# Reordering four short schedules around retention and the first merge tiles of a hybrid decoder step

## The chip, the core and the metric

The program runs on one core of a Trainium2 chip, in float32. The core has a matrix engine (TensorE, PE in the profile), a vector engine (VectorE, DVE), an activation engine (ScalarE, ACT), a general engine (GpSimd, POOL) and a queue engine that issues most of the transfers (SyncE, SP). Each engine runs its own instruction list in order, and they meet only at semaphores. The metric is the device time of one execution in microseconds.

## What is computed

One step of one decoder layer, for a prompt of 512 tokens (with 16 meta tokens ahead of them) and 8 single-token samples. The normalised input is projected once into the inputs of four token mixers: A differential attention, B retention, C a short convolution with a gated linear recurrence, D gated linear attention. Each mixer's output goes through its own projection and is gated by a sigmoid of another projection of the input:

```
gates = sigmoid(xn @ w_merge + b_merge)          # one gate per branch and channel
proj  = einsum('blnw,nwd->blnd', [oa, ob, oc, od], w_branch)
hres  = x + sum(gates * proj) @ w_out
y     = hres + hier_moe(rms_norm(hres))          # top-1 group, top-2 experts in it
```

Three parts matter here. Retention (B) of the prompt is `o = ((q k^T) * decay) v`, followed by a group norm (subtract the mean, divide by the deviation) and a gate. For the samples, attention (A) reads a paged cache of 2048 past keys and values per sample; the scores are `sum over d of q[d] * k[d]`. Mixer D needs exponentials of differences of cumulative log-decays.

## The kernel before

**The streams.** PE is given one hand-written order, the list `PROJ` and the list `PAIRS`. First come the input projections, one weight chunk per tile (DQ, DK, CR0 to CI1, DV0, DV1, DR0, DR1, DA are the last of them), each tile made of two halves of eight matmuls (sixteen rows of the profile, 128x268). Between and behind the halves PE does a step of another job. During DK, DV and DR these are the ten steps of prompt retention, `retention_step(r)`: PE multiplies the decayed scores of step r-1 with the values (L703) and makes the raw scores of step r (L696), two score units a step. Raw scores of 512, 400, 272, 144 and 16 columns belong to r = 0 to 4 and again to r = 5 to 9. DVE's `decayed(u)` (L1801) multiplies a unit's scores with the decay table and frees PE to go on: `ret_out(u)` on PE waits for it. After DR1 come the transposed keys (L725, L728), DVE's decayed keys (L1859, L1862) and then PE's `ret_states` (L738), which waits for DVE's last one.

**The cached keys.** For the samples' scores the cache is cut into 32 units (8 samples, two halves, two parts each). A unit's pages are fetched by SP in `cache(j)` (two units per call, L404, with the sample's own key row at L407 when the half is the second), multiplied with the query by POOL (L2396) and summed by DVE (`sample_scores`, L1775). DVE's sum waits for POOL's product of that very unit (`k_mul`); SP's transfer of unit x waits until the unit four before it was summed (`k_used`). Every fourth unit, 23 and 27 and 31 among them, has 1280 columns, the others 1024. How many units DVE sums at which place is written by hand: `K_BESIDE` during attention (15 units in all), `K_RET[r]` behind retention step r, and then two times `K_TAIL` = 3. `K_AFTER[j - 2]` names the PE tile behind whose ring slot SP puts `cache(j)`: first all weight chunks whose slot is free by that tile, then the cache call.

**Means and the tiles behind them.** After the last projections PE does the first two merge tiles, GC0/PC0 and GC1/PC1. Behind PC0 stand the two group-norm means of retention (BMEAN0, BMEAN1, at L554) and the log-decays (LA); behind PC1 the two variances (BVAR0, BVAR1). PSUM banks alternate between these tiles, and `pj_free` counts the evictions, in order, that a tile two places later waits for. In `ret_means`, ACT waits for DVE's centring (`b_cen`, L1892) and counts the two evictions for it, then evicts LA, squares, and makes the softplus of the log-decays. POOL, at unit `K_LAST` = 26, stores three states and waits for `g_t` 3, DVE's third group of sums of the input (L1876, L1878, L1881).

**The product stage.** From there every pair of gate tiles is made from seven products (X1, X6, X7, X5, X2, X4, X3 in PE's order, L841) with five `adds` on DVE (U, V, 22, 21, 12; L1995 to L2015), and two branch tiles (L810) follow. X3 waits for the second add of 22, the first branch tile for the first add of 21, the second branch tile for the add 12. In the second pair (q = 1) DVE does in between `arguments(0, 0)` to `(0, 2)` (L1840 to L1850), which prepare the exponentials of mixer D; `exp_sums` (L1921), behind them, is waited for by a matmul of PE at L1001.

## Time and profile before

| | |
|---|---|
| runs of the kernel before | 852.36, 852.52, 851.33 us; median 852.36 |
| the profiled execution | 852.36 us, with a span of 850.6 us |
| PE busy | 799.4 us, 94% of the span |
| DVE busy | 384.6 us, 45% |
| ACT busy | 225.6 us, 27% |
| POOL busy | 281.6 us, 33% |
| mean granted clock of PE | 0.973 of full speed |

The span runs from the first to the last instruction of the profile; 1.8 us of the execution lie outside it. A share of busy time is a mean over all stages. Whoever wants to know what a stage is worth has to look at the idle gaps of the engine that is nearly always busy, at what ended each of them, and at how far ahead the other engines are at that place.

### The profile page before, as it was taken

Reading aid. Unit: us, or ns where it says so; the run is one execution under the profiler, and the core shown is the slowest. Engines: PE = TensorE matmul, PEld = TensorE weight load, DVE = VectorE, ACT = ScalarE, POOL = GpSimd, SP = SyncE. Lnnn points to the kernel's source line nnn. Section 1 sums busy time; section 2 is a strip of 40 time slices with the busy share of each in tenths; the row PEclk is TensorE's granted clock in tenths of the full one; section 3 lists DMA queues with packets and bytes.
Section 4 is the critical chain, followed back from the end, with each engine's and each line's share of the span. In section 5 each row is a group of like instructions: output and inputs, shape, how many; then the busy total and the mean of one; then the engine's idle time right before and its main releaser. Section 6 shows DMA issues by size and latency. Waiting matters only on the chain. (4 is left out here: it accounts for less than half of the span.)

```text
span 850.6 us, 14296 instructions
## 1 busy us (share of the span) xinstructions
PE 799.4 (94%) x5314; PEld 568.2 (67%) x5314; DVE 384.6 (45%) x700; ACT 225.6 (27%) x427; POOL 281.6 (33%) x204
## 2 busy tenths in 40 slices
PE   9999999989999998999999999999999799999970
PEld 8887777666677786777767778888887533333320
DVE  4671676657488599545554111633312612112010
ACT  4122333331422634132403224222102412112010
POOL 0000511344564784355434546431000113332303
PEclk9999989989999999999999999999999799999986
DMA  9243622245565432435444542332095679999942
GB/s 368 92 136 111 203 85 77 82 138 153 162 186 185 150 118 67 129 111 170 147 136 136 182 141 87 106 120 86 28 320 212 211 277 379 363 371 366 352 143 35
DMA packets 85450, 147.23 MB, mean 173 GB/s; under 512 B 13063, under 2 KB 46872, under 8 KB 85252
## 3 DMA queue, kind: packets, MB, share of 16 engines
q1 hardware_dynamic: 79012, 135.42, 47.3%
q0 software_dynamic: 5920, 10.82, 5.0%
q8 instruction: 42, 0.69, 0.3%
q14 instruction: 28, 0.23, 0.1%
q10 hardware_dynamic: 448, 0.06, 0.1%
HBM read 137.71 MB, written 18.90 MB: 184 GB/s over the span
## 5 line engine op out<-in xcount | busy, mean ns | idle before, releaser
L565 PE MATMUL ps<-xn,ring 128*128 128x268 f32 (+1 forms) x576 | 138.7, 396 | 1.0 <-ACT qb L1302 0.9
L565 PEld LDWEIGHTS ps<-xn,ring 128*128 128x128 f32 x576 | 108.5, 192 | 26.2 <-issue 3.4
L2396 POOL TENSOR_TENSOR kv<-kv,sgd 128x1024 f32<-128x1024 f32 (+1 forms) x32 | 80.9, 2542 | 124.1 <-DVE tmp L1742 72.8
L1445 ACT ACTIVATE sgt<-sgt,vec 128x260 f32<-128x260 f32 x60 | 30.1, 510 | 142.4 <-DVE sgt L2004 79.4
L2486 POOL DMA_INDIRECT out_y<-cst,gtab x24 | 37.3, 1555 | 82.8 <-DVE cst L2321 50.7
L810 PE MATMUL ps<-br,ring 128*128 128x260 f32 x256 | 61.7, 388 | 2.1 <-DVE sgt L2008 1.3
L841 PE MATMUL ps<-xn,ring 128*128 128x260 f32 x240 | 58.8, 388 | 2.3 <-ACT cst L1302 1.3
L841 PE MATMUL ps<-xn,qb 128*128 128x260 f32 x240 | 57.7, 383 | 0.0
L1048 PE MATMUL ps<-qk,ring 128*128 128x260 f32 x256 | 56.5, 383 | 0.0
L810 PEld LDWEIGHTS ps<-br,ring 128*128 128x128 f32 x256 | 47.6, 190 | 12.8 <-issue 2.8
L1048 PEld LDWEIGHTS ps<-qk,ring 128*128 128x128 f32 x256 | 48.6, 190 | 7.8 <-issue 0.4
L841 PEld LDWEIGHTS ps<-xn,ring 128*128 128x128 f32 x240 | 44.4, 190 | 13.0 <-issue 6.5
L841 PEld LDWEIGHTS ps<-xn,qb 128*128 128x128 f32 x240 | 45.3, 190 | 7.1
L1775 DVE TENSOR_REDUCE sgd<-kv 128x32 f32<-128x1024 f32 (+1 forms) x32 | 40.4, 1279 | 9.3 <-POOL kv L2396 9.2
L2309 DVE TENSOR_TENSOR ring<-ring,ps 128x256 f32<-128x256 f32 x12 | 5.1, 421 | 71.1 <-ACT ring L1596 69.9
L2435 POOL TENSOR_TENSOR qb<-ring 128x512 f32<-128x512 f32 x15 | 25.0, 1666 | 31.3 <-PE ps L841 31.0
L2440 POOL TENSOR_TENSOR qb<-qb,ring 128x512 f32<-128x512 f32 x15 | 20.0, 1336 | 45.0 <-PE ps L841 45.0
L1995 DVE TENSOR_TENSOR sgt<-ps,sgt 128x260 f32<-128x260 f32 x15 | 6.4, 427 | 61.5 <-PE ps L841 61.5
L608 PE MATMUL ps<-ring,xn 128*128 128x128 f32 x256 | 32.6, 292 | 0.0
L608 PEld LDWEIGHTS ps<-ring,xn 128*128 128x128 f32 x256 | 32.1, 207 | 0.6 <-ACT tmp L1302 0.3
L2447 POOL TENSOR_TENSOR qb<-ring,qb 128x512 f32<-128x512 f32 x15 | 20.0, 1333 | 34.8 <-PE ps L841 34.8
L2407 POOL TENSOR_TENSOR cst<-sgt,cst 128x520 f32<-128x520 f32 x16 | 20.6, 1285 | 31.8 <-ACTq L1450 31.8
(464 smaller groups left out, 1317.7 us busy)
## 6 DMA issues: line engine op xcount, KB each, us to landing
ring<-in_w_mg SPq DMA_DIRECT2D x32, 640.0 KB, 4.4
kv<-in_kc SPq DMA_DIRECT2D x128, 128.0 KB, 2.2
kv<-in_vc SPq DMA_DIRECT2D x128, 128.0 KB, 2.1
ring<-in_w_in SPq DMA_DIRECT2D x24, 512.0 KB, 4.6
kv<-in_w SPq DMA_DIRECT2D x8, 1024.0 KB
br<-in_w SPq DMA_DIRECT2D x8, 1024.0 KB, 17.4
sgd<-in_w SPq DMA_DIRECT2D x8, 1024.0 KB, 16.6
qk<-in_w SPq DMA_DIRECT2D x6, 1024.0 KB, 15.3
```

The lines of the kernel that those rows point to most:

```text
L565: mm = pe.matmul(ps[:, 2 * (t % 2) + h, 0:hw], wsl(c, k), xnv[:, k, col0 + h * hw:col0 + (h + 1) * hw], start=(k == 0), stop=(k == KT - 1))
L608: pe.matmul(ps[:, 2 * (t % 2), b * P:(b + 1) * P], xnv[:, k, b * P:(b + 1) * P], wsl(c, k), start=(k == 0), stop=(k == KT - 1))
L810: mm = pe.matmul(ps[:, bk + h, 0:HN], wsl(CAT[f"G{n}{m}"], KT + k), brv[:, BR[n] + k, h * HN:(h + 1) * HN], start=(k == 0), stop=(k == 1))
L841: mm = pe.matmul(ps[:, bk, 0:HN], w[:, k * P:(k + 1) * P], x, start=(k == 0), stop=(k == 3))
L1048: mm = pe.matmul(ps[:, 2 * (m % 2) + h, 0:HN], ring[:, s0:s0 + P], acc[:, k, h * HN:(h + 1) * HN], start=(k == 0), stop=(k == KT - 1))
L1445: act.activation(g, g, ACT.Sigmoid, bias=vv(V_BM + 8 * "ABCD".index(n) + m + i)).then_inc(g_a, 1)
L1775: dve.tensor_reduce(row, kb.rearrange("p s (m d) -> p s m d", d=32), X, ALU.add).then_inc(k_used, 1)
L2396: pool.tensor_tensor(kb, kb, qbc[:, b:b + 1, :].to_broadcast([P, HALF // 2 + (half and u), 256]), ALU.mult)\
L2407: link(pool.tensor_tensor(p_, g, p_, ALU.mult))
L2435: pool.tensor_tensor(s1, half_of(b, 0), half_of(b, 1), ALU.add).then_inc(g_s, 1)
L2440: pool.tensor_tensor(s2, s1, half_of(a, 0), ALU.subtract).then_inc(g_s, 1)
L2486: pool.indirect_dma_start(out=o["y"], out_offset=on_rows(to), in_=rows.rearrange("p a n -> p (a n)"), in_offset=None, bounds_check=N - 1, ...
```

## The change

Five edits, all of them in order or in waiting; no matmul is added or moved.

1. `K_RET` changes from [0, 0, 1, 2, 2, 1, 1, 0, 1, 3] to [0, 0, 1, 2, 2, 2, 2, 0, 0, 2]: the same 11 units, with units 21 and 22 each one place earlier, unit 23 behind step 6 and no longer behind step 9.
2. `K_AFTER`: `cache(12)`, `cache(13)` and `cache(14)` are each issued one weight chunk earlier.
3. POOL no longer waits for `g_t` 3 ahead of unit 26.
4. The two means are copied from PSUM by ACT into `bsd`, which counts the eviction; DVE subtracts from there. ACT waits for the centring later, ahead of its squares.
5. In the second pair, each `arguments(0, k)` stands one place earlier among the adds.

```diff
-K_AFTER = ["BK1", "BG0", "BG1", "V3", "CX1", "CG0", "CG1", "DQ", "DQ", "DK", "DV0", "DV1", "DR0"]
+K_AFTER = ["BK1", "BG0", "BG1", "V3", "CX1", "CG0", "CG1", "DQ", "DQ", "DK", "DK", "DV0", "DV1"]
...
-K_RET = [0, 0, 1, 2, 2, 1, 1, 0, 1, 3]
+K_RET = [0, 0, 1, 2, 2, 2, 2, 0, 0, 2]
...
                 for t in range(2):
-                    act.wait_ge(b_cen, t + 1)
-                    act.sem_inc(pj_free, 1)
+                    copy(f"BMEAN{t}", bsd[:, t, :], HN)
                 act.activation(fold(dg[:, 0, :], HT), pair("LA", HT), ACT.Identity, bias=vv(V_GB)).then_inc(pj_free, 1)
                 for t in range(2):
+                    act.wait_ge(b_cen, t + 1)
                     act.activation(bn[:, t, :], brv[:, 2 + t, :], ACT.Square).then_inc(b_sq, 1)
...
             for t in range(2):
-                dve.wait_ge(pj, AT[f"BMEAN{t}"] + 1)
-                bk = BANK[f"BMEAN{t}"]
-                tt(fold(brv[:, 2 + t, :], HN), fold(brv[:, 2 + t, :], HN), ps[:, bk:bk + 2, 0:HN], ALU.subtract).then_inc(b_cen, 1)
+                dve.wait_ge(pj_free, EV[f"BMEAN{t}"] + 1)
+                tt(brv[:, 2 + t, :], brv[:, 2 + t, :], bsd[:, t, :], ALU.subtract).then_inc(b_cen, 1)
...
+            arguments(0, 0)
             adds(1, "22")
-            arguments(0, 0)
+            arguments(0, 1)
             adds(1, "21")
-            arguments(0, 1)
+            arguments(0, 2)
             adds(1, "12")
-            arguments(0, 2)
             exp_sums()
...
                     pool.dma_start(o["c"], cst_out).then_inc(outs, 16)
-                    pool.wait_ge(g_t, 3)
```

On DVE, in retention steps 5 to 8, the kernel before has this order. L1801 with 512, 400, 272 and 144 columns is the decay multiplication of steps 5, 6, 7 and 8; L1775 is the sum of one unit, 128x40 being a unit of 1280 columns; L1826 to L1828 belong to mixer C.

```order
L1801 TENSOR_TENSOR tmp<-ps,cst 128x512 [waits at_o,at_s] x2
L1775 TENSOR_REDUCE sgd<-kv 128x32 [waits k_mul]
L1801 TENSOR_TENSOR tmp<-ps,cst 128x400 [waits at_o,at_s] x2
L1775 TENSOR_REDUCE sgd<-kv 128x32 [waits k_mul]
L1801 TENSOR_TENSOR tmp<-ps,cst 128x272 [waits at_o,at_s] x2
L1826 TENSOR_TENSOR qk<-qk,qb 128x1072 [waits c_act]
```

The changed kernel has this at the same place:

```order
L1801 TENSOR_TENSOR tmp<-ps,cst 128x512 [waits at_o,at_s] x2
L1775 TENSOR_REDUCE sgd<-kv 128x32 [waits k_mul] x2
L1801 TENSOR_TENSOR tmp<-ps,cst 128x400 [waits at_o,at_s] x2
L1775 TENSOR_REDUCE sgd<-kv 128x32 [waits k_mul]
L1775 TENSOR_REDUCE sgd<-kv 128x40 [waits k_mul]
L1801 TENSOR_TENSOR tmp<-ps,cst 128x272 [waits at_o,at_s] x2
```

The sums of units 22 and 23 now stand ahead of the decay multiplication of step 7; the sum of unit 23 (128x40) waits there for POOL's product of that unit.

On DVE in the second pair of the product stage the kernel before has this order. L2004 and L2005 are the two adds of 22, L2008 and L2011 those of 21, L2015 is 12; L1840 to L1850 are the arguments.

```order
L2004 TENSOR_TENSOR sgt<-ps,sgt 128x260
L2005 TENSOR_TENSOR sgt<-ps,sgt 128x260
L1840 COPY tmp<-ea 128x512
L1841 TENSOR_TENSOR tmp<-ea 128x512
L1845 TENSOR_TENSOR ea<-ea 128x256
L2008 TENSOR_TENSOR sgt<-ps,sgt 128x260
L2011 TENSOR_TENSOR sgt<-ps,sgt 128x260
L1840 COPY tmp<-ea 128x512
L1841 TENSOR_TENSOR tmp<-ea 128x512
L1845 TENSOR_TENSOR ea<-ea 128x128x2
L2015 TENSOR_TENSOR sgt<-ps,sgt 128x260
```

In the changed kernel (its line numbers behind the edits are one lower) it reads:

```order
L1840 COPY tmp<-ea 128x512
L1841 TENSOR_TENSOR tmp<-ea 128x512
L1845 TENSOR_TENSOR ea<-ea 128x256
L2003 TENSOR_TENSOR sgt<-ps,sgt 128x260
L2004 TENSOR_TENSOR sgt<-ps,sgt 128x260
L1840 COPY tmp<-ea 128x512
L1841 TENSOR_TENSOR tmp<-ea 128x512
L1845 TENSOR_TENSOR ea<-ea 128x128x2
L2007 TENSOR_TENSOR sgt<-ps,sgt 128x260
L2010 TENSOR_TENSOR sgt<-ps,sgt 128x260
```

Each group of adds has moved behind one more group of arguments; the last one, with its scan of 16 columns (L1848) and two small operations, now stands ahead of the add 12.

## Rows read from the trace of the kernel before

**Rows 1.** The page: busy time of PE (its first item), whole span
```profile
PE 799.4 (94%) x5314; PEld 568.2 (67%) x5314; DVE 384.6 (45%) x700; ACT 225.6 (27%) x427; POOL 281.6 (33%) x204
```
**Rows 2.** Waits of PE, 240 to 370 us: total, times, longest
```profile
PE ps L1001 <- DVE sgd L1921: 1.8, 1, 1.8
...
PE ps L738 <- DVE tmp L1862: 0.8, 1, 0.8
PE ps L810 <- DVE sgt L2015: 0.8, 1, 0.8
```
**Rows 3.** Timeline of SP: start, us, engine, line, transfer, count
```profile
233.46 6.25 SPq L404 DMA_DIRECT2D kv<-in_kc  x8
239.75 0.32 SPq L407 DMA_DIRECT2D kv<-scr_qk  x1
...
252.08 8.46 SPq L404 DMA_DIRECT2D kv<-in_kc  x8
```
**Rows 4.** Timeline of POOL: the products of units 23 and 31
```profile
241.69 3.78 POOL L2396 TENSOR_TENSOR kv<-kv,sgd 128x1280 f32<-128x1280 f32 x1 [2.19 <-DMA kv<-scr_qk]
...
281.56 2.91 POOL L2396 TENSOR_TENSOR kv<-kv,sgd 128x1280 f32<-128x1280 f32 x1 [0.80 <-DMA kv<-scr_qk]
```
**Rows 5.** Timeline of DVE during retention; in brackets idle before, and its end
```profile
239.44 0.79 DVE L1801 TENSOR_TENSOR tmp<-ps,cst 128x272 f32<-128x272 f32 x2 [3.11 <-PE ps L696]
...
241.44 1.27 DVE L1827 TENSOR_TENSOR qb<-br 128x1072 f32<-128x1072 f32 x1
242.75 3.86 DVE L1828 SCALAR_TENSOR_TENSOR cx<-qb,cx 128x1072 f32<-128x1072 f32 x1
...
256.64 3.73 DVE L1775 TENSOR_REDUCE sgd<-kv 128x40 f32<-128x1280 f32 x3
...
284.51 1.49 DVE L1775 TENSOR_REDUCE sgd<-kv 128x40 f32<-128x1280 f32 x1 [1.18 <-POOL kv L2396]
```
**Rows 6.** Timeline of PE, retention steps 7 to 9, variances, X3 of pair 1
```profile
243.15 0.68 PE L703 MATMUL ps<-tmp,vtok 128*64 128x272 f32 x4
...
244.20 3.88 PE L565 MATMUL ps<-xn,ring 128*128 128x268 f32 x16
...
290.04 2.06 PE L554 MATMUL ps<-tmp,cst 128*128 128x260 f32 x8
...
320.15 1.92 PE L841 MATMUL ps<-xn,qb 128*128 128x260 f32 x8
```
**Rows 7.** Stretches: length, busy of each engine, then PEclk, DMA share, GB/s
```profile
125.00:130.00 5.00, 5.00 (x30) 4.88 (x29) 2.71 (x9) 1.96 (x8) 0.00 (x0) 0.56 0.00 0
324.00:332.00 8.00, 5.60 (x29) 4.68 (x30) 7.68 (x10) 4.40 (x6) 2.57 (x2) 1.00 0.51 164
```
**Rows 8.** Timeline of PE around a gap during attention
```profile
121.50 1.92 PE L640 MATMUL ps<-qk 32*128 32x512 f32 x8 [1.88 <-DVE br L1748]
123.36 6.69 PE L608 MATMUL ps<-ring,xn 128*128 128x128 f32 x32
...
133.68 3.73 PE L608 MATMUL ps<-ring,xn 128*128 128x128 f32 x32
```
**Rows 9.** Timeline of ACT: eviction of GC1
```profile
289.05 0.69 ACT L1302 ACTIVATE sgt<-ps,vec 128x520 f32<-128x520 f32 x1
```
**Rows 10.** Timeline of DVE: first add of pair 0, adds and arguments of pair 1
```profile
296.87 0.43 DVE L1995 TENSOR_TENSOR sgt<-ps,sgt 128x260 f32<-128x260 f32 x1 [6.19 <-PE ps L841]
...
319.19 0.70 DVE L1840 COPY tmp<-ea 128x512 f32<-128x512 f32 x1
319.81 0.68 DVE L1841 TENSOR_TENSOR tmp<-ea 128x512 f32<-128x512 f32 x1
320.52 0.43 DVE L1845 TENSOR_TENSOR ea<-ea 128x256 f32<-128x256 f32 x1
...
324.12 0.43 DVE L2015 TENSOR_TENSOR sgt<-ps,sgt 128x260 f32<-128x260 f32 x1
...
328.91 2.08 DVE L1921 TENSOR_REDUCE sgd<-sgd 128x64 f32<-128x1088 f32 x1
```

## The prediction

> **What bounds the kernel now.** Start with the page: PE is busy for 799.4 of 850.6 us [rows 1], so the time is PE's list plus its gaps. Next ask for PE's waits between 240 and 370 us, where all five edits lie. Three of them end on DVE: 0.8 us ahead of the states of retention, 0.8 us ahead of a branch tile, 1.8 us at L1001 [rows 2]. Together 3.4 us, the most that these edits could win. Then read the timelines of SP, POOL, DVE and PE side by side, to see how far ahead each helper is of the place where PE needs it. A moved step is free only if it fits in that lead. Behind this region I expect PE to pass a shift on: the waits of its product stage hang on work that itself starts at PE's products.
>
> **The sums moved forward in retention (K_RET).** This decides the case. DVE sums unit 23 now between retention steps 6 and 7 and must first have POOL's product of it. SP had that unit's last transfer out at 239.75 + 0.32 = 240.07 us [rows 3], and POOL began at 241.69 us, when it had landed [rows 4]. Nothing in the change brings this forward: the chunks move only behind that call, and SP was issuing without a break, as its eight issues of 6.25 us show beside the one call that did wait, 8.46 us [rows 3]. POOL's product took 3.78 us there, since it began while DVE's L1827 ran, until 242.71 us [rows 4, 5]; the same form takes 2.91 us undisturbed [rows 4], and DVE stands still in the changed kernel, so I take 2.91. Then: product done at 241.69 + 2.91 = 244.60; its sum, 1.49 us [rows 5], at 246.1; the first of the two decay multiplications, half of 0.79 us [rows 5], at 246.5. PE wants that result at 243.15 us [rows 6]. It stands 246.5 - 243.15 = **3.4 us**. Before, DVE did that multiplication at 239.44 us [rows 5] and PE never waited. The bounds: with the product at 3.78 us it is 4.2; were transfer and product each some tenths quicker, 2.9.
>
> Queued behind DVE's waiting sum are the decay multiplications, mixer C's L1826 to L1828 and so its recurrence. L1828 took 3.86 us, ending 1.1 us after POOL's product [rows 4, 5]; now it would meet no product and end some 2.5 us sooner, so that mixer C loses about as much as PE, not more, and the decay of step 8 stays hidden under the half of 3.88 us that PE does first [rows 6].
>
> **What a gap of 3.4 us does to PE's clock.** Around 121 us PE stood 1.88 us, among small matmuls [rows 8]. The granted clock then was 0.56 of full speed from 125 to 130 us [rows 7], that is the lower level (1.2 of 2.4 GHz) for 4.4 of the 5 us, and a group of 32 matmuls took 6.69 us where the same group took 3.73 later [rows 8]: 3.0 us lost. The gaps of 0.8 and 1.8 us around 324 to 332 us left the clock at 1.00 [rows 7]. So gaps of near 1.9 us fall on either side, and one of 3.4 us, followed by 0.7 us of small matmuls [rows 6], lies well past them. I take the fall and **3.0 us**; the bounds are 0 and, with some loss in the work ahead of such a group, 3.4.
>
> **The states (L738).** DVE reached the decayed keys late, since three sums of together 3.73 us stood ahead of them [rows 5]. With two, and PE 6.4 us later, it is there first: DVE's chain from the decay of step 9 to the keys loses only PE's shift and is shorter by the sum of unit 23 at least. The wait goes: **-0.8 us**; it is 0 at worst if POOL's products of units 24 and 25, late because of mixer C, are in the way.
>
> **SP and POOL (K_AFTER, g_t).** One chunk issue is 0.35 to 0.4 us, so three cache calls come that much earlier. The 2 us that SP stood in the call at 252.08 us (8.46 against 6.25 [rows 3]), because unit 23 was not yet summed, go as well. Neither is on PE's path: the last units' sums are followed on DVE by a stand of 6.19 us [rows 10]. Without the wait for g_t, POOL starts unit 26 about 1.2 us sooner in relation to DVE and collides with its sums of the input. **0**, covered by those 6.19 us ahead of DVE's first add; without that cover it would cost up to one product, 2.4 us.
>
> **The means.** Two more evictions on ACT, into time in which it waited for PE. PE no longer depends on DVE for the two banks, but did not wait for them before either, so there is nothing to win. What can be lost: the subtraction now reads two operands in SBUF. L1828, of that kind, ended 1.1 us behind POOL's product though it was issued 2.7 us before its end [rows 4, 5]: such an operation stands until the product is over. POOL's last products, of units 28 to 31, run at that place, and PE's shift brings the subtraction under the last of them. ACT's squares wait for it, and behind these ACT evicts GC1, done at 289.05 + 0.69 = 289.74 us, for the variance matmul at 290.04 us [rows 6, 9]: 0.3 us of lead, and some 1 us more ahead of the second square. A product of 2.91 us in the way would leave a wait of about 1.8 us, none leaves 0; whether the last product is in flight just then hangs on tenths, so I take the middle, **+0.9 us**. The bounds are 0 and 2.6.
>
> The Trainium skill ("SBUF — State Buffer", section "SBUF: two separate sides") says that a VectorE operation with two SBUF inputs and a GpSimd operation take one shared port pair in turn, each for its whole length. By that rule the mean subtraction is exposed where reading PSUM was not, and the wait would be nearer to its upper bound; the trace agrees, with 3.86 us for L1828 against 1.27 us for its like-sized neighbour.
>
> **The arguments in pair 1.** DVE is the late engine here. The first three argument operations cost 0.70 + 0.68 + 0.43 = 1.8 us [rows 10] and now stand ahead of the adds of 22. These were over when the first copy began, at 319.2 us, 0.9 us before PE began X3 at 320.15 us [rows 6, 10]; now at 321.1 + 0.8 = 321.9: X3 stands 1.8 us. The second group holds the adds of 21 until about 324, another 0.3 us ahead of the first branch tile. The third group, with its scan, was 328.8 - 324.5 = 4.3 us, of which some 1.5 to 2 us fell under POOL's work (as L1828 did); it now lies ahead of the add 12, which ends near 327.6 us instead of 324.55 us. PE's second branch tile starts 3.1 us later than before. In return L1921 still ends near 329.8 us against 330.99 us before [rows 10], and PE, later itself, does not wait for it: 1.8 us back [rows 2]. 3.1 - 1.8 is 1.3, and 0.3 us of a later short wait go: **+1.0 us**. The bounds: if POOL's work happens not to meet the arguments, the adds are 2 us sooner and the sum is -0.8; 1.3 above.
>
> **The sum.** The profiled execution took 852.36 us, equal to the median. 852.36 + 3.4 + 3.0 - 0.8 + 0 + 0.9 + 1.0 = 859.9 us.
>
> **The rivals.**
> - *The clock does not fall in retention.* Everything else as above: 856.9 us. For it: the 1.8 us gap without a fall [rows 7]. Against: the gap here is nearly twice that.
> - *The clock falls a second time, in pair 1.* PE would stand 1.8, 0.3 and 1.8 us within 6 us there; the two gaps of before, 0.8 and 1.8 us, left it alone [rows 7], a single one of 1.88 us did not [rows 8]. Another 3.0 us: 862.9 us.
> - *The sum of unit 23 is not waited for*, and the result is faster. It decides where the product ends: it had to be done by 243.15 - 0.4 - 1.49 = 241.3 us, and it starts only at 241.69 us [rows 4]. If it were, the gap and the clock's fall would go, the wait of 0.8 us with them, and with arguments at their lower bound (-0.8) and no collision at the means: 852.36 - 0.8 - 0.8 = 850.8 us, 848.9 if all 3.4 us of [rows 2] went. Only a much faster transfer would do it, against the row.
> - *The edits cancel*, within 0.2%: a wait of 1 to 2 us in retention without a fall of the clock, and the wins of the arguments: about 853 us.
>
> **How the numbers follow.** Chances: forecast 0.50 (by itself 858 to 861.8), no fall of the clock 0.19, second fall 0.18, cancelled 0.08, faster 0.05. About 0.2%, 1.7 us, is what a measurement of this kernel can tell from no change. So faster has 0.05, same 0.08, slower 0.87. The range must leave out two tenths: faster and cancelled, 0.13, and the upper part of the second fall, where the collision at the means is at its bound as well. It reaches from 854.5, under the no-fall case with small arguments, to 864.0 us.
>
> **What would show it.** PE's waits: a new one of 3 to 4 us at L703 near 243 us, released by DVE's L1801, behind a DVE gap released by POOL's L2396. The stretch from 246 to 253 us: granted clock under 0.8, and a half of sixteen matmuls taking more than 6 us instead of 3.88. No wait at L738. A wait at X3 (L841) and at both branch tiles near 326 to 335 us, and none at L1001. The forecast is wrong if POOL's product of unit 23 is over by 241 us, or if PE goes through step 7 without a gap; then look first at SP's issue times of that unit.

## The result, and the profile after

Eight runs of the changed kernel gave a median of 856.9 us (854.7 to 860.2); eight of the kernel before, a median of 850.9 us (847.1 to 852.5). The ratio is 1.0073, with a 95% interval of 1.0048 to 1.0098: about 6.2 us slower. All 27 executions of the changed kernel on record lie between 852.3 and 860.8 us. Two slow executions of the kernel before, of 864.8 and 1370.7 us in the first set of experiments below, are left out of the ratios. The profiled execution of the changed kernel took 858.98 us, with a span of 857.2 us. PE is busy nearly as long as before [rows 1]:

```profile
PE 800.2 (93%) x5314; PEld 569.6 (66%) x5314; DVE 382.9 (45%) x700; ACT 227.2 (27%) x429; POOL 279.3 (33%) x204
```

"Busy" holds slow matmuls too, so this row says little: a microsecond lost to the clock counts as work. PE's waits between 225 and 380 us of the changed kernel say more. They stand beside [rows 2]; the columns are total, times and longest (line numbers behind the edits are one or two lower than in the kernel before):

```profile
PE ps L554 <- ACT sgt L1302: 3.7, 1, 3.7
PE ps L703 <- DVE tmp L1801: 3.6, 1, 3.6
PE ps L810 <- DVE sgt L2014: 2.1, 1, 2.1
PE ps L841 <- DVE sgt L2004: 1.6, 1, 1.6
```

Two of the three old waits are gone (L738 and L1001, together 2.6 us), and the four listed add up to 11.0 us. They begin three separate losses.

**Retention.** With the new `K_RET` unit 22 is summed behind step 6 as well, where it was behind step 8. POOL and DVE of the changed kernel, around the sum of unit 23 (against [rows 4, 5]):

```profile
239.14 2.89 POOL L2394 TENSOR_TENSOR kv<-kv,sgd 128x1280 f32<-128x1280 f32 x1 [1.85 <-DMA kv<-scr_qk]
```
```profile
242.06 1.49 DVE L1775 TENSOR_REDUCE sgd<-kv 128x40 f32<-128x1280 f32 x1 [3.52 <-POOL kv L2394]
243.46 0.78 DVE L1801 TENSOR_TENSOR tmp<-ps,cst 128x272 f32<-128x272 f32 x2
...
246.77 1.27 DVE L1828 SCALAR_TENSOR_TENSOR cx<-qb,cx 128x1072 f32<-128x1072 f32 x1
```

PE at that place, the twin of [rows 6], and two stretches of it (length, busy of each engine, then PEclk, DMA share, GB/s):

```profile
231.15 3.88 PE L565 MATMUL ps<-xn,ring 128*128 128x268 f32 x16
...
243.95 1.52 PE L703 MATMUL ps<-tmp,vtok 128*64 128x272 f32 x4 [3.62 <-DVE tmp L1801]
245.40 0.85 PE L696 MATMUL ps<-qk 64*128 64x144 f32 x4
246.18 5.57 PE L565 MATMUL ps<-xn,ring 128*128 128x268 f32 x16
```
```profile
240.00:245.00 5.00, 1.38 (x6) 0.58 (x4) 2.94 (x4) 1.90 (x2) 2.03 (x1) 0.78 0.42 107
245.00:250.00 5.00, 5.00 (x16) 3.49 (x14) 3.41 (x5) 1.10 (x1) 1.88 (x1) 0.54 0.76 235
```

The chain reads without a break: POOL's product ends at 242.03, the sum at 243.55, the first of the two decay multiplications at about 243.9, and PE goes on at 243.95 after 3.62 us. The granted clock then falls to 0.54 of full speed, the lower level (1.2 GHz) for most of that stretch. L703 takes 1.52 us (0.68 before), L696 0.85 (0.52) and the half behind them 5.57 (3.88): 2.9 us. Some 0.3 us of this are not the clock's: in the run only_ret below L703 took 1.02 us behind its wait although the granted clock stayed at 1.00.

**Means and variances.** POOL, then DVE, ACT and PE of the changed kernel:

```profile
270.62 15.03 POOL L2394 TENSOR_TENSOR kv<-kv,sgd 128x1024 f32<-128x1024 f32 x6
285.62 1.26 POOL L2433 TENSOR_TENSOR qb<-ring 128x512 f32<-128x512 f32 x1
```
```profile
282.81 6.31 DVE L1891 TENSOR_TENSOR br<-br,tmp 128x520 f32<-128x520 f32 x2 [3.39 <-ACT tmp L1302]
```
```profile
287.48 0.64 ACT L1483 ACTIVATE tmp<-br 128x520 f32<-128x520 f32 x1 [2.72 <-DVE br L1891]
289.16 0.64 ACT L1483 ACTIVATE tmp<-br 128x520 f32<-128x520 f32 x1 [1.05 <-DVE br L1891]
...
295.67 0.69 ACT L1302 ACTIVATE sgt<-ps,vec 128x520 f32<-128x520 f32 x1
```
```profile
296.51 2.93 PE L554 MATMUL ps<-tmp,cst 128*128 128x260 f32 x8 [3.68 <-ACT sgt L1302]
```

Here are the last six products in one row of 15.03 us. The first new subtraction begins at 282.81 us, where the fifth of them gives way to the sixth, and lets ACT's square go only at 287.48 us, behind the last product and a further operation of POOL (285.62 to 286.88 us). The two subtractions took 4.63 and 1.76 us, where the old form took 0.70 us each. ACT stands 2.72 + 1.05 us; everything behind it moves, and the eviction of GC1 ends at 296.36 us, not at 289.74 [rows 9]. PE stands 3.68 us where it had not waited, and its clock falls again: PEclk is 0.76 from 295 to 302 us.

**Pair 1.** DVE and PE of the changed kernel, against [rows 6, 10]:

```profile
325.34 1.37 DVE L1840 COPY tmp<-ea 128x512 f32<-128x512 f32 x1
...
328.16 0.42 DVE L2004 TENSOR_TENSOR sgt<-ps,sgt 128x260 f32<-128x260 f32 x1
...
334.13 0.43 DVE L2014 TENSOR_TENSOR sgt<-ps,sgt 128x260 f32<-128x260 f32 x1 [0.21 <-DVE ea L1850]
```
```profile
328.72 1.99 PE L841 MATMUL ps<-xn,qb 128*128 128x260 f32 x8 [1.55 <-DVE sgt L2004]
330.55 1.96 PE L810 MATMUL ps<-br,ring 128*128 128x260 f32 x8
334.62 3.53 PE L810 MATMUL ps<-br,ring 128*128 128x260 f32 x8 [2.11 <-DVE sgt L2014]
```

X3 stands 1.55 us, the second branch tile 2.11 us, and that tile then runs at the lower clock level for most of its 3.53 us (PEclk is 0.66 from 335 to 340 us).

**Where the time stood at each place.** The start of the same work of PE, in both traces, in us:

| PE's work | before | after | difference |
|---|---|---|---|
| half behind retention step 6 (L565) | 234.04 | 231.15 | -2.9 |
| values of step 7 (L703) | 243.15 | 243.95 | +0.8 |
| values of step 8 | 248.01 | 251.68 | +3.7 |
| states (L738) | 262.00 | 264.77 | +2.8 |
| first variance (L554) | 290.04 | 296.51 | +6.5 |
| second product of pair 0 (L841) | 294.92 | 301.78 | +6.9 |
| second branch tile of pair 1 (L810) | 324.61 | 334.62 | +10.0 |
| L841 behind L1001 | 331.32 | 340.96 | +9.6 |
| L1108, ahead of the experts | 670.48 | 679.74 | +9.3 |
| an expert matmul (L1206) | 783.88 | 795.95 | +12.1 |
| last group of L1206 | 828.85 | 835.70 | +6.9 |

The region of the edits lost 12.5 us (from -2.9 to +9.6), twice what the whole lost. Three microseconds had been won ahead of it, by no edit: the granted clock during attention fell less in this execution (0.95 from 126 to 134 us and 1.00 from 182 to 190, against 0.79 and 0.88 in the kernel before). Behind L1108 the lag first grew by 2.8 us, among it a wait of 1.4 us for weights that the kernel before did not have. Then 5.2 us came back at the end of the experts. PE in the kernel before, near its end, waits and runs slow there:

```profile
820.01 1.94 PE L1206 MATMUL ps<-sgd,cx 128*32 128x512 f32 x8 [1.44 <-DMA sgd<-in_w]
821.72 3.64 PE L1206 MATMUL ps<-br,cx 128*32 128x512 f32 x16
825.14 2.17 PE L1206 MATMUL ps<-sgd,cx 128*32 128x512 f32 x16
```

and the changed kernel, at the same place:

```profile
829.66 1.06 PE L1206 MATMUL ps<-sgd,cx 128*32 128x512 f32 x8 [1.44 <-DMA sgd<-in_w]
830.54 1.90 PE L1206 MATMUL ps<-br,cx 128*32 128x512 f32 x16
```

The slow clock cost the kernel before 0.9 + 1.7 + 0.3 = 2.9 us there. Its waits for weights in this last stretch were 0.9 + 1.6 + 1.4 = 3.9 us, those of the changed kernel 0.3 + 1.4 = 1.7 us. Together that is 5.1 of the 5.2 us.

### The profile page after: what moved, and what is told of

Same layout as the page of the kernel before. It is cut to its first block and busy times, and to the rows that moved or that the text cites. A ratio compares the mean times of both kernels' runs of the same rounds, so it can differ in the third digit from the quotient of the medians.

```text
span 857.2 us, 14295 instructions
## 1 busy us (share of the span) xinstructions
PE 800.2 (93%) x5314; PEld 569.6 (66%) x5314; DVE 382.9 (45%) x700; ACT 227.2 (27%) x429; POOL 279.3 (33%) x204
## 5 line engine op out<-in xcount | busy, mean ns | idle before, releaser
L565 PE MATMUL ps<-xn,ring 128*128 128x268 f32 (+1 forms) x576 | 140.0, 399 | 1.0 <-ACT qb L1302 0.9
L565 PEld LDWEIGHTS ps<-xn,ring 128*128 128x128 f32 x576 | 109.3, 194 | 26.8 <-issue 3.7
L2394 POOL TENSOR_TENSOR kv<-kv,sgd 128x1024 f32<-128x1024 f32 (+1 forms) x32 | 79.1, 2489 | 121.4 <-DVE tmp L1742 70.2
L810 PE MATMUL ps<-br,ring 128*128 128x260 f32 x256 | 63.2, 395 | 3.4 <-DVE sgt L2014 2.1
L841 PE MATMUL ps<-xn,ring 128*128 128x260 f32 x240 | 59.5, 391 | 1.3 <-ACT cst L1302 1.3
L841 PE MATMUL ps<-xn,qb 128*128 128x260 f32 x240 | 57.8, 384 | 1.6 <-DVE sgt L2004 1.6
L810 PEld LDWEIGHTS ps<-br,ring 128*128 128x128 f32 x256 | 48.3, 193 | 14.6 <-issue 2.8
L841 PEld LDWEIGHTS ps<-xn,ring 128*128 128x128 f32 x240 | 45.0, 193 | 12.2 <-issue 5.5
L841 PEld LDWEIGHTS ps<-xn,qb 128*128 128x128 f32 x240 | 45.1, 190 | 9.0 <-issue 1.9
L1775 DVE TENSOR_REDUCE sgd<-kv 128x32 f32<-128x1024 f32 (+1 forms) x32 | 40.6, 1280 | 19.7 <-POOL kv L2394 19.7
L1948 DVE COPY_PREDICATED vtok<-cst,ps 128x1024 f32<-128x1024 int32 x16 | 20.9, 1305 | 22.2 <-PE ps L910 22.2
```

What stands on the lines that cost most here:

```text
L565: mm = pe.matmul(ps[:, 2 * (t % 2) + h, 0:hw], wsl(c, k), xnv[:, k, col0 + h * hw:col0 + (h + 1) * hw], start=(k == 0), stop=(k == KT - 1))
L810: mm = pe.matmul(ps[:, bk + h, 0:HN], wsl(CAT[f"G{n}{m}"], KT + k), brv[:, BR[n] + k, h * HN:(h + 1) * HN], start=(k == 0), stop=(k == 1))
L841: mm = pe.matmul(ps[:, bk, 0:HN], w[:, k * P:(k + 1) * P], x, start=(k == 0), stop=(k == 3))
L1775: dve.tensor_reduce(row, kb.rearrange("p s (m d) -> p s m d", d=32), X, ALU.add).then_inc(k_used, 1)
L1948: dve.copy_predicated(am[:, 2 * hp:2 * hp + 2, :, :].rearrange("p h i t -> p (h i) t"), mask.unsqueeze(1).to_broadcast([P, 8, P]), ps[:, 6 ...
L2394: pool.tensor_tensor(kb, kb, qbc[:, b:b + 1, :].to_broadcast([P, HALF // 2 + (half and u), 256]), ALU.mult)\
```

## The experiments

Twelve kernels were run, in three sets, each beside 27 to 35 runs of the kernel before (medians 849.6, 849.8 and 849.8 us). Each kernel was run twelve times, undo_ret ten times and undo_args six times. A ratio is always against the kernel before; it is estimated from the single runs and is not exactly the quotient of two medians. Single runs of every kernel are spread over 4 to 10 us, so a ratio carries some 0.2% of uncertainty, and a profiled execution need not be a typical one.

| kernel | median us | ratio | 95% interval |
|---|---|---|---|
| changed kernel | 856.9 | 1.0073 | 1.0048 to 1.0098 |
| undo_ret | 853.0 | 1.0044 | 1.0030 to 1.0058 |
| undo_means | 855.1 | 1.0071 | 1.0047 to 1.0096 |
| undo_args | 857.6 | 1.0092 | 1.0069 to 1.0114 |
| only_ret | 853.6 | 1.0035 | 1.0015 to 1.0054 |
| ret_filled | 853.6 | 1.0036 | 1.0017 to 1.0054 |
| only_loads | 855.4 | 1.0063 | 1.0043 to 1.0082 |
| only_means | 851.6 | 1.0006 | 0.9988 to 1.0024 |
| only_args | 851.7 | 1.0010 | 0.9993 to 1.0028 |
| only_gt | 853.9 | 1.0051 | 1.0031 to 1.0070 |
| only_kafter | 848.8 | 0.9993 | 0.9978 to 1.0008 |
| loads_means | 851.8 | 1.0030 | 1.0010 to 1.0050 |
| both_early | 851.0 | 1.0018 | 0.9998 to 1.0038 |

The theory before these runs was that of the prediction: the sum of unit 23 in retention carries the loss, with a fall of the clock behind it. The rivals: means and arguments carry it, or the loads.

### Undo one edit at a time

**undo_ret**: the changed kernel with the old places of the sums.

```diff
-K_RET = [0, 0, 1, 2, 2, 2, 2, 0, 0, 2]
+K_RET = [0, 0, 1, 2, 2, 1, 1, 0, 1, 3]
```

> The changed kernel with the old K_RET (unit 23 summed behind retention step 9 again); the other four edits stay. My theory: the gap of 3.6 us at L703 and the clock's fall behind it go, so PE comes to the means about 6 us earlier than in the changed kernel. The mean subtraction then meets POOL's products of units 29 to 31 at another phase: a wait at L554 for the variance of 0 to 3 us. Pair 1 keeps its waits at X3 and the second branch tile. In all 2 to 5 us above the kernel before (ratio 1.002 to 1.006). Rival, that the retention step is nothing by itself and the means and arguments alone make the loss: no change against the changed kernel, 1.007.

Measured 1.0044: some 2.5 us of the 6 are gone, fewer than the prediction's terms for this edit (3.4 + 3.0 - 0.8 = 5.6 us). The gap at L703 is gone, 0.8 us at L738 are back, and 1.0 us are left of the 3.7 at L554. Pair 1 waits 2.0 and 2.1 us. But a thing that I had not foreseen stands in DVE's timeline of this kernel, beside POOL's:

```profile
264.28 10.60 DVE L1881 TENSOR_TENSOR sgd<-xn,cx 128x520 f32<-128x520 f32 x1
274.81 0.69 DVE L1881 TENSOR_TENSOR cst<-xn,cx 128x520 f32<-128x520 f32 x1
```
```profile
264.49 9.82 POOL L2394 TENSOR_TENSOR kv<-kv,sgd 128x1024 f32<-128x1024 f32 x4
```

An addition that takes 0.69 us takes 10.60: it ends only when POOL's four products, issued without a break, are over. In the changed kernel the same addition began at 268.17 us and took 0.70, since POOL's products began only at 270.62. So undoing one edit uncovered the cost of another, and the undo doesn't price `K_RET` alone.

**undo_means**: the changed kernel with the means in their old form (the fourth edit of the change taken back).

```diff
-                    copy(f"BMEAN{t}", bsd[:, t, :], HN)
+                    act.wait_ge(b_cen, t + 1)
+                    act.sem_inc(pj_free, 1)
...
-                tt(brv[:, 2 + t, :], brv[:, 2 + t, :], bsd[:, t, :], ALU.subtract).then_inc(b_cen, 1)
+                tt(fold(brv[:, 2 + t, :], HN), fold(brv[:, 2 + t, :], HN), ps[:, bk:bk + 2, 0:HN], ALU.subtract).then_inc(b_cen, 1)
```

> The changed kernel with the old means (DVE subtracts straight from PSUM, ACT waits for it); the rest stays. My theory: the subtraction from PSUM takes 0.7 us whatever POOL does, so the 3.7 us wait of PE at the first variance goes, and DVE's 6.31 us for two subtractions become 1.4. The gap in retention stays at 3.6 us. Time 2 to 4 us under the changed kernel, ratio to before 1.003 to 1.005. Rival, that ACT was late for another reason (its two new evictions): the 3.7 us wait stays in the trace with the subtractions at 0.7 us each.

Measured 1.0071, the same as the changed kernel within the intervals and not the 1.003 to 1.005 expected, although the wait of 3.7 us at L554 is gone from its trace. The gap in retention is 1.8 us there and not 3.6 (see only_ret). DVE's two subtractions, now with one operand in PSUM, under the last of POOL's six products:

```profile
279.43 0.70 DVE L1892 TENSOR_TENSOR br<-br,ps 128x520 f32<-128x520 f32 x1 [4.38 <-PE ps L554]
280.39 0.70 DVE L1892 TENSOR_TENSOR br<-br,ps 128x520 f32<-128x520 f32 x1 [0.26 <-PE ps L554]
```
```profile
266.27 15.01 POOL L2395 TENSOR_TENSOR kv<-kv,sgd 128x1024 f32<-128x1024 f32 x6
```

They are not held up at all: 0.70 us each under a running product, against 6.31 us for the two of the changed kernel. That shows the mechanism, and ACT's new evictions, the rival, are not the cause. What it is worth in the median this run does not show: its twelve runs lie between 849.7 and 859.2 us, and the profiled one, 851.3, is among the four shortest.

**undo_args**: the changed kernel with the arguments in their old places.

```diff
-            arguments(0, 0)
             adds(1, "22")
-            arguments(0, 1)
+            arguments(0, 0)
             adds(1, "21")
-            arguments(0, 2)
+            arguments(0, 1)
             adds(1, "12")
+            arguments(0, 2)
```

> The changed kernel with the old place of the arguments in pair 1; the rest stays. My theory: the waits of 1.6 us at X3 and 2.1 us at the second branch tile go and 0.8 and 1.8 us of before come back, and the clock does not fall near 335 us; 2 to 3 us under the changed kernel, ratio to before 1.004 to 1.005. Rival, that the arguments are neutral (what they cost ahead of X3 they give back at L1001): no change against the changed kernel, 1.007.

Measured 1.0092, in six runs: not faster than the changed kernel, so the expected win of 2 to 3 us did not come. Its waits are those expected (3.7 at L554, 3.4 at L703, 0.8 at L810, 1.8 at L1001), and the two waits of pair 1 are gone. But the clock, which was not to fall here, fell behind L1001: the eight matmuls after it took 3.43 us, 1.97 in the kernel before. The intervals of this kernel and the changed one overlap, so no gain from the moved arguments is shown either.

### One edit alone

**only_ret**: the kernel before with the new K_RET alone.

```diff
-K_RET = [0, 0, 1, 2, 2, 1, 1, 0, 1, 3]
+K_RET = [0, 0, 1, 2, 2, 2, 2, 0, 0, 2]
```

> The kernel before with only the new K_RET. My theory: the gap of 3.6 us at L703, the clock's fall behind it (about 2.9 us), no wait at the states (-0.8 us): 4 to 6 us above the kernel before, ratio 1.005 to 1.007. Rival, that the gap comes back later from slack: under 1.002.

Measured 1.0035, 3.0 us, less than the 1.005 to 1.007 expected. Its profiled execution was the shortest of its twelve (849.4 to 856.0), and shows a reason: POOL's product, then PE.

```profile
237.09 2.89 POOL L2396 TENSOR_TENSOR kv<-kv,sgd 128x1280 f32<-128x1280 f32 x1 [1.50 <-DMA kv<-scr_qk]
```
```profile
241.91 1.02 PE L703 MATMUL ps<-tmp,vtok 128*64 128x272 f32 x4 [1.77 <-DVE tmp L1801]
...
243.30 3.88 PE L565 MATMUL ps<-xn,ring 128*128 128x268 f32 x16
```

Here POOL began the product 3.05 us ahead of the point at which PE wanted the decayed scores (241.91 - 1.77 = 240.14), in the changed kernel 1.2 us ahead of it (240.33 against 239.14), in the kernel before 1.5 us ahead [rows 4, 6]. The chain of product, sum and decay is the same, near 4.8 us; the gap is the rest. It is 1.8 us in one execution and 3.6 in another. Four traces with this edit show both kinds: gaps of 3.62 (changed kernel) and 3.38 us (undo_args), each with the clock near 0.5 behind them and L565 at 5.57 and 5.81 us; gaps of 1.77 (here) and 1.83 us (undo_means), each with the clock at 1.00 and L565 at 3.88 us. The edit costs what the prediction said in the one phase and, by my estimate, about 1 us (1.8 less the 0.8 of L738) in the other. The phase is set ahead of the edit. SP's call for units 20 and 21, the one before, took 7.50 and 7.85 us in the two traces with the long gap and 6.20 and 6.21 us in those with the short one, and the call for units 22 and 23 began that much later. Why that call is longer in some executions no run shows; the kernel before had the long one too (7.28 us), so one profile of it could only show the long phase.

**ret_filled**: only_ret, and seven more matmuls' worth of work (their result is not used) ahead of PE's values of step 7.

```diff
+                if r == 8:
+                    t, c = AT["DR0"], CAT["DR0"]
+                    free(t)
+                    loaded(c)
+                    for k in range(7):
+                        pe.matmul(ps[:, 2 * (t % 2), 0:HT], wsl(c, k), xnv[:, k, 0:HT], start=True, stop=True)
```

> As only_ret, with seven extra matmuls of 268 columns (fourteen rows of the profile, 3.4 us at full clock) on PE at the place of the gap, written to a free bank of PSUM and overwritten by the next tile. PE waits as long as in only_ret but is busy. Theory, that 2.9 us of the loss come from the clock and not from the wait: the granted clock stays at 1.00 from 240 to 252 us, the next group of sixteen matmuls takes 3.88 us, and the time is 2 to 3 us under only_ret, ratio to before 1.002 to 1.004. Rival, that the matmuls behind the gap are slow for another reason (transfers, the bank): they stay at 5.5 us and the time is that of only_ret or more.

PE of this kernel (L719 is the filling; lines behind it have numbers six higher) and its stretch behind the place:

```profile
241.49 3.33 PE L719 MATMUL ps<-xn,ring 128*128 128x268 f32 x14
244.74 0.68 PE L703 MATMUL ps<-tmp,vtok 128*64 128x272 f32 x4
...
245.80 3.88 PE L565 MATMUL ps<-xn,ring 128*128 128x268 f32 x16
```
```profile
245.00:250.00 5.00, 5.00 (x28) 3.46 (x24) 2.92 (x4) 1.10 (x1) 2.39 (x2) 1.00 0.73 224
```

No gap is left, and the clock stays at 1.00. But the test is weaker than it was meant to be. POOL began the product at 238.62 us in this execution, 3.0 us ahead of PE's need (241.65), so it was one of the short phase: without the filling the gap would have been near 1.8 us (an estimate from its own rows), and behind such a gap at this place the clock stayed up in both traces that have one. The run shows that the delay can be filled and the clock then stays up, not that filling prevents a fall that would have come. The ratio, 1.0036, is that of only_ret: 3.3 us of filling in every execution cost as much as a gap that is short in some and long, with a fall, in others.

**only_loads**: the kernel before with the second and the third edit.

```diff
-K_AFTER = ["BK1", "BG0", "BG1", "V3", "CX1", "CG0", "CG1", "DQ", "DQ", "DK", "DV0", "DV1", "DR0"]
+K_AFTER = ["BK1", "BG0", "BG1", "V3", "CX1", "CG0", "CG1", "DQ", "DQ", "DK", "DK", "DV0", "DV1"]
...
-                    pool.wait_ge(g_t, 3)
```

> The kernel before with K_AFTER changed and POOL's wait for g_t 3 taken out, nothing else. My theory: neither is on PE's path; cache calls 12 to 14 come 0.4 us earlier, POOL's unit 26 about 1.2 us earlier, and the ratio is 1.000, at most 0.002 from it. Rival, that POOL's earlier start pushes DVE's sums of the input and later sums behind its products: a new wait of PE at the states or at the first means, and 1.002 or more.

Measured 1.0063, 5.4 us: the dearest of the edits by itself, where I had put 0. DVE, and then PE:

```profile
264.43 10.62 DVE L1881 TENSOR_TENSOR sgd<-xn,cx 128x520 f32<-128x520 f32 x1
...
277.73 3.67 DVE L1775 TENSOR_REDUCE sgd<-kv 128x32 f32<-128x1024 f32 x3
281.32 1.28 DVE L1892 TENSOR_TENSOR br<-br,ps 128x520 f32<-128x520 f32 x2
```
```profile
282.10 2.15 PE L849 MATMUL ps<-ea,vec 128*128 128x268 f32 x4 [4.51 <-ACTq L1480]
284.05 9.17 PE L565 MATMUL ps<-xn,ring 128*128 128x260 f32 x32
```

Again 10.62 us for an addition of 0.7. Three sums and the centring (L1892) come late; ACT counts the bank of the mean only behind the centring, and the log-decays' matmul (L849) needs the bank. PE stands 4.51 us, and the next tile takes 9.17 us, against 7.24 in the kernel before, with the granted clock at 0.50 from 282 to 286 us. The rival of the expectation, that POOL's earlier start pushes DVE's work behind its products, is what happened.

**only_means** and **only_args**: the kernel before with the fourth edit, and with the fifth (the diffs are those of the change).

> The kernel before with only the new means. My theory: the subtractions meet POOL's products of units 30 and 31, since in the kernel before DVE centres at 279.4 and 280.4 us and POOL multiplies until 284.4 us with one short pause: DVE takes 3 to 6 us for the two instead of 1.4, ACT's squares come 1 to 3 us late, PE waits 1 to 3 us for the variance: ratio 1.001 to 1.004. Rival, that the collision needs the shift that K_RET makes: no wait, 1.000.

> The kernel before with only the arguments moved. My theory: X3 waits 1.6 us, the second branch tile 2.1 us, L1001 no longer 1.8 us, and the clock may fall behind it as it did near 337 us: 1 to 3 us above before, ratio 1.001 to 1.003. Rival, that it is neutral or wins: 0.999 to 1.000.

Measured 1.0006 and 1.0010: neither can be told from no change, though each interval leaves room for some 2 us. With the means alone POOL's five products are over at 278.35 us, so that the subtractions meet the last one only briefly, DVE in only_means:

```profile
277.64 1.88 DVE L1891 TENSOR_TENSOR br<-br,tmp 128x520 f32<-128x520 f32 x2 [2.66 <-ACT tmp L1302]
```

PE has no wait at L554 then: the collision needs the shift that the other edits make, as the rival said. With the arguments alone PE waits 1.6 us at X3 and 2.1 at the second branch tile, as in the changed kernel, and not at L1001; the clock falls behind the second wait here as well (0.71 from 325 to 330 us).

### What the loads cost, taken apart

The theory after this first half: POOL's wait for `g_t` 3 was a fence. It kept the products behind DVE's third group of sums; without it four of them hold DVE back. The rival: it takes the earlier transfers as well, since four products in a row need four units in place.

**only_gt**: the kernel before without the wait.

```diff
-                    pool.wait_ge(g_t, 3)
```

> The kernel before with one edit: POOL does not wait for g_t 3 ahead of unit 26. Theory P (the wait for g_t kept POOL's four products and DVE's third group of sums apart): the second operation of L1881 lies under several products, about 10.6 us instead of 1 to 2, PE has a new wait of 3 to 4.5 us at L849 released by ACT's queue at L1480, slow matmuls behind it, ratio about 1.006. Theory Q (it takes the earlier loads too, so that four products are ready in a row): L1881 ends after one product, no wait at L849, ratio 1.000 to 1.001.

**only_kafter**: the kernel before with the earlier cache calls and the wait kept.

```diff
-K_AFTER = ["BK1", "BG0", "BG1", "V3", "CX1", "CG0", "CG1", "DQ", "DQ", "DK", "DV0", "DV1", "DR0"]
+K_AFTER = ["BK1", "BG0", "BG1", "V3", "CX1", "CG0", "CG1", "DQ", "DQ", "DK", "DK", "DV0", "DV1"]
```

> The kernel before with the three cache calls one chunk earlier and POOL's wait for g_t kept. Theory P: the wait holds unit 26 back until DVE's third group is done; no wait at L849; waits of PE as in the kernel before (0.8 at L738, 0.8 at L810, 1.8 at L1001), ratio 0.999 to 1.001. Rival: the earlier loads alone bring the products under DVE's sums of the input, wait at L849 of some us, ratio 1.003 to 1.006.

only_gt measured 1.0051, only_kafter 0.9993. DVE and PE of only_gt:

```profile
266.90 10.61 DVE L1881 TENSOR_TENSOR sgd<-xn,cx 128x520 f32<-128x520 f32 x1
```
```profile
284.55 1.17 PE L849 MATMUL ps<-ea,vec 128*128 128x268 f32 x4 [2.81 <-ACTq L1480]
```

and DVE, then POOL, of only_kafter:

```profile
265.35 0.70 DVE L1881 TENSOR_TENSOR sgd<-xn,cx 128x520 f32<-128x520 f32 x1
```
```profile
266.75 9.87 POOL L2396 TENSOR_TENSOR kv<-kv,sgd 128x1024 f32<-128x1024 f32 x4 [1.21 <-DVE cst L1881]
```

The wait at L849 is 2.81 us and not the 4.51 of only_loads because PE came to it later: its tile ahead of that place took 8.97 us, 7.28 in the kernel before, at a granted clock of 0.57 from 269 to 273 us and without a wait in front of it. Both directions are shown. The removed wait alone makes the stall, and with the wait kept four products in a row do no harm: they stand 1.21 us for DVE and then run where DVE has nothing of that kind to do. The earlier loads cost nothing. The rival falls.

**loads_means**: only_loads with the new means (the two hunks of only_loads, and the means as in the change). It asks whether the new eviction of the means, by ACT and not counted behind DVE, shields PE from a late DVE.

> The kernel before with K_AFTER, without the wait for g_t and with the new evictions of the means. Theory: DVE is held at L1881 for some 10 us as with the loads alone, but PE no longer depends on DVE for the two banks, so the wait of 4.5 us at L849 is gone or under 1 us and the slow matmuls with it; ratio 1.000 to 1.003, against 1.0063 without the new means. Rival: the lateness of DVE shows itself further on instead (squares, variances at L554), a wait of 2 to 4 us there, ratio 1.004 to 1.007.

Measured 1.0030, against 1.0063 without the new means; the intervals overlap a little. DVE is held for 10.60 us as before, PE has no wait at L849, but it has one further on:

```profile
289.16 1.99 PE L554 MATMUL ps<-tmp,cst 128*128 128x260 f32 x8 [2.66 <-ACT sgt L1302]
```

The shield works for the bank and not for the squares, as the rival expected: the lateness shows itself at L554, where 2.66 us are left of 4.51, with no slow tile ahead (7.24 us).

### A version from what was learnt

**both_early**: the kernel before with only one sum moved, unit 23 behind step 8, where its product is there; the earlier loads with the wait for `g_t` kept; and `exp_sums` ahead of the third arguments.

```diff
-K_RET = [0, 0, 1, 2, 2, 1, 1, 0, 1, 3]
+K_RET = [0, 0, 1, 2, 2, 2, 1, 0, 1, 2]
...
+            exp_sums()
             arguments(0, 2)
-            exp_sums()
```

> A candidate built from what the runs showed: the kernel before with K_RET [0, 0, 1, 2, 2, 2, 1, 0, 1, 2] (one sum earlier, unit 23 behind step 8, where its product is ready), the cache calls one chunk earlier with the wait for g_t kept, and exp_sums ahead of arguments(0, 2). If it holds: no wait at L703, none at L738 (0.8 won), none at L1001 (1.8 won), the rest as before; ratio 0.997 to 0.999. Rival (the weights' stream sets the end of the expert part, so that PE's lead is given back): waits gone, ratio 0.999 to 1.001. Against: a new collision at the means or at L849, 1.002 or more.

Measured 1.0018 (0.9998 to 1.0038). All waits that it was to remove are gone: none at L703, L738, L1001. But the ratio is not the 0.997 to 0.999 hoped for. A new wait stands on PE, 15 us behind, and the eight matmuls after it (L841) took 3.67 us, 2.02 in the kernel before:

```profile
342.14 1.16 PE L910 MATMUL ps<-tmp 32*128 32x128 f32 x16 [2.24 <-DVE vtok L1949]
```

DVE did the same work in another order, and PE met it at the next place where it needs DVE. No version faster than the kernel before was found; only_kafter, at 0.9993, is the same within its interval.

## Why the prediction came out right, and where it did not

859.9 us were forecast for the profiled execution, between 854.5 and 864.0; it took 858.98, and the median is 856.9. The direction and the size are right, the size partly by luck. The gap, the fall of the clock and the states came out in this trace as summed up; the terms for POOL, for the means and for the arguments did not.

- **The gap in retention, 3.4 us: right in this trace.** It is 3.62 us, with each link as worked out: product 2.89 (2.91 taken), sum 1.49, half of 0.78. L1828 met no product, 1.27 us against 3.86, as said. What the step missed is that it is not a constant of the kernel: POOL's product began at another moment against PE, and in only_ret the gap was 1.8 us. (Lead and gap add up to 4.8 us in each trace.) One profile gave one phase, and I read it as the only one. Taken alone the edit costs 3.0 us in the median, where gap, fall and the freed wait were to give 5.6.
- **The fall of the clock, 3.0 us: right in this trace, 2.9 us.** Four traces go together at this place: a fall behind each of the two long gaps, none behind the two short ones. An experiment that separates the gap from the fall at the long phase was not had, since ret_filled met the short one. That gaps of near 1.9 us "fall on either side" is borne out by L1001 (see the last section).
- **The states, -0.8 us: right.** No wait at L738, and PE's lag shrank by 0.9 us there.
- **POOL without the wait, 0: this step failed.** The prediction said "covered by those 6.19 us ahead of DVE's first add" and bounded the cost at one product, 2.4 us. Both were wrong. The lead was read at the last sum, while the work that is hit has an earlier user: DVE's centring, and behind it the bank that L849 needs. And a VectorE operation was let wait for one product where it waited for four. By itself the edit costs 0.5%. In the changed kernel the cost does not appear, and that was not foreseen either: DVE, with one sum fewer ahead of the keys, was at L1881 at 268.17 us, while POOL was held by ACT's states until 269.45 us and multiplied only from 270.62 us. `K_RET`, the other harmful edit, hid this one: of the seven traces without the wait for `g_t`, the three with the new `K_RET` (changed kernel, undo_means, undo_args) have L1881 at 0.70 us and the four without it at 10.6. So the 0 in the sum met the result by luck, and not for the reason given.
- **The means, +0.9 us: mis-sized.** The mechanism is right, the squares waited and L554 behind them, but it was 3.7 us and outside the bound of 2.6. The bound was one product of 2.91 us; the first subtraction was held from 282.81 to about 287.4 us, by what was left of the products and one more POOL operation. The clock fell behind the wait as well, for which the sum had no term: L554 took 2.93 us (2.06 before) and X1 2.71 (1.99), and in return X1's own wait of 1.0 us went. The whole step at this place is +4.1 us (from +2.8 to +6.9), where 0.9 was forecast. In the median the edit shows nothing, neither alone nor undone: in only_means the subtractions met POOL only briefly.
- **The arguments, +1.0 us: the waits nearly right, the clock missing.** X3 stood 1.55 us (1.8 forecast), L1001 nothing (as forecast). The 1.8 was luck: the working adds the 0.8 us of the two adds a second time (they were over at 319.2 us, so 1.8 us of arguments gives 321.0 us and a wait of 0.9), and leaves out that the first copy, L1840, took 1.37 us and not 0.70, beside an operation of POOL that began 0.25 us ahead of it. The net step of this pair in the trace is +2.7 us (from +6.9 to +9.6), since the second branch tile ran mostly at the lower clock: 3.53 us, 1.5 more than before. That is the fall of the rival with a second fall in pair 1, which I gave 0.18; it cost about half of its 3.0 us. The edit alone is worth 0.1%, which can't be told from nothing.
- **"PE passes a shift on" held up to the experts, not through them.** The lag was 9.3 us at L1108 and 6.9 us at the last group of L1206. The kernel before had a slow stretch behind a wait for weights that the changed one did not have. No experiment tests whether the longer lead of the weights caused that; it stays open.

So the region lost 12.5 us where 7.5 were forecast, and some 6 us that I had no term for lay on the other side: 2.9 us ahead of the edits, most of it the clock during attention, and a net 2.7 us in the clock and the waits of the experts. The profiled execution also stood 2 us above the median. That the sum met the whole to 1 us is to that extent luck. A forecast of the whole can be near for less good reasons than it seems; the single terms have to be looked at.

The Trainium skill ("SBUF — State Buffer", section "SBUF: two separate sides") says that such a VectorE operation and a GpSimd operation share one port pair, each holding it for its whole length. The traces agree as to which operations are concerned: 0.70 us with an operand in PSUM (undo_means), 6.31 us for two with both in SBUF (changed kernel), each beside the last of POOL's six products. I had read "in turn" into it; the trace shows no turns.

## What to carry to other kernels

A wait that no result depends on may be a fence between two engines that disturb each other; before removing it, ask what the freed engine will run beside, and for how many operations in a row. Read the lead at the first user of the work that is delayed, not at the last. And price a step moved ahead of a producer by the phase between the two engines in several executions, since one profile shows only one; where an edit hides another's cost, single edits and undone edits do not add up (1.0035, 1.0063, 1.0006 and 1.0010 alone, 1.0073 together).

## What the hardware showed that I had not expected

- A VectorE addition of two SBUF operands, 0.70 us by itself, took 10.60 to 10.62 us in four kernels (undo_ret, only_loads, only_gt, loads_means) when POOL issued four products without a break from 0.2 us behind its start. It was not let in between them, although its own record begins first.
- The length of a wait of PE does not settle by itself whether the clock falls behind it. One wait, 1.80 us at L1001, stands in nine traces. In four of them the eight matmuls behind it took 3.4 to 3.6 us, in five 1.97 us. PE of only_kafter there, to be set beside 1.97 us in the kernel before:

```profile
329.21 0.43 PE L1001 MATMUL ps<-sgd,cst 128*128 128x64 f32 x2 [1.80 <-DVE sgd L1921]
329.48 3.51 PE L841 MATMUL ps<-cx,qb 128*128 128x260 f32 x8
```

- In the retention, mean and pair stages of these traces the clock fell behind each of the five longest waits (3.38, 3.62, twice 3.68, 4.51 us), and in all four traces in which PE stood 1.6 to 2.0 us at X3 and 2.1 us again two tiles later. It stayed up behind the single ones of 2.66 (loads_means) and 2.81 us (only_gt), and fell behind one of 2.24 us (both_early).
- In four of the fourteen traces (undo_ret, undo_means, ret_filled, only_gt) it fell between 265 and 273 us, to 0.57 to 0.64 in stretches of 3 to 4 us, behind the 64 one-column matmuls of L747 and no wait above 0.8 us. In the other ten it stayed at 1.00 behind the same matmuls. What decides it no run shows.
- Two executions of nearly the same work differ by 3 us ahead of the first edit, most of it by falls of the clock: 0.79 against 0.95 from 126 to 134 us, 0.88 against 1.00 from 182 to 190 us.
